# A block of hybrid layers, a two-way recurrence and routed experts on one core: layer fronts renewed, and the recurrence's products joined and reordered

## The chip, the core and the metric

The kernel runs on one core of a Trainium2 chip. The metric is the device time of one execution in microseconds (us), the median of several runs. TensorE (PE) multiplies matrices into PSUM banks, VectorE (DVE), ScalarE (ACT) and GpSimd (POOL) work on what lies in SBUF and PSUM, and SyncE (SP) issues most DMA transfers. Each engine executes its own instructions in order, and semaphores tie them together.

## What is computed

Two hybrid layers (convolution, retention and windowed attention over 256 tokens of width 1024), a mixer with a recurrence over a context and a latent sequence of 256 tokens each, and 32 experts. What the change touches is the head of each layer and the recurrence:

```python
def rms_norm(x, g):
    xf = x.astype(jnp.float32)
    y = xf * lax.rsqrt(jnp.mean(xf * xf, axis=-1, keepdims=True) + EPS) * g.astype(jnp.float32)
...
def hybrid_layer(x, ...):
    h = rms_norm(x, norm_g)
    z = h @ w_in
...
def wkv_bidir(r, k_d, v, kk, w, a, state0):
    ...
    def step(s, inp):
        r_t, w_t, k_t, v_t, aa_t, bb_t = inp
        sa = jnp.einsum('dbhij,dbhj->dbhi', s, aa_t)
        s = s * w_t[..., None, :] + sa[..., :, None] * bb_t[..., None, :] + v_t[..., :, None] * k_t[..., None, :]
        y_t = jnp.einsum('dbhij,dbhj->dbhi', s, r_t)
        return s, y_t
    state, ys = lax.scan(step, state0, xs)
```

The recurrence has 8 heads of 64 and two directions (d). It runs over the context first, and its final states start the latent one.

## The kernel before

All is float32. A loop over two layers (hybrid_tensor, hybrid_scalar, hybrid_pool, hybrid_vector, hybrid_loads; one function per engine) is followed by the mixer and then by a loop over experts. Weights come in units of 2 MB (1024 x 512) through a ring of three buffers, issued by SyncE in the order in which TensorE uses them. The order on every engine is that of the code; nothing is scheduled by a planner.

**The front of a layer.** ScalarE squares xT in four pieces, TensorE sums the squares with a matrix of ones (L305), ScalarE takes the root (L532), VectorE the reciprocal (L699), and eight operations scale xT into hT (L706), one per 128 features. After the last of them h_ready rises, and TensorE begins the first unit of the projection (features, L265). Between the sums and this unit TensorE has the products of ada(0) (L231). ScalarE works by function tables; where the next function lies in another table, an ACT_TABLE_LOAD stands ahead of it. The parameters of a layer, par, are loaded by GpSimd at its start into one buffer (L659), after the last addition to xT of the layer before; ScalarE waits for them ahead of the root, because the exponential of lam (L527) reads them and stands there. All engines wait at the program's start for four transfers: xT, shared_cons, cons and mpar.

**The recurrence.** It goes by chunks of 64 tokens: four turns over the context (turns 0 to 3) and four over the latent (4 to 7). The tokens of a chunk are tied by a triangular system, which is inverted by doubling in five levels. All is done for two directions and four pairs of heads, so a product is a group of 16 matmuls of 64x64 (helper halves, L1381): for each of the four pairs c and each direction d the upper and the lower half of the partitions. both_ways issues it with d innermost. In most products direction 1 is turned: its upper half of partitions goes to the lower half of PSUM and the other way round. In g0_state, out_state and d0 it is not. Within the kernel's names:

- front: pairs (B by A, masked by VectorE into MP, L2124) and firsts (A by B, from which the first inverse is made, L2128 and L2131). The front of turn n + 1 is issued in turn n behind the product u, except at the change to the latent.
- a level k: t1 (T1 = level cut by X1, banks 0 and 1), copied by ScalarE (L1802), then d1 (banks 2 and 3), which VectorE adds to X1 (L2181), and d0 (banks 4 and 5), which accumulates X0 and which ScalarE copies (L1794). GpSimd makes the level cuts from MP (L1208).
- between(k) stands between t1 and d1: the products of keys, more, g0_state, g0_keys, state_keys and out_state. In latent turns a fill (beside: work of other parts, L1496 to L1509) follows, and TensorE waits for it.
- by_token: V, B and K of the chunk are transposed by products with the identity (L1423), ahead of t1 of levels 1, 2 and 3, into tV, tB and tK. VectorE copies V for it into sV (L2106).
- aside: in context turns ScalarE and VectorE do work for the latent part between the steps of a level.

Each t1, d1 and d0 waits for both directions of what it reads:

```python
    pe.wait_ge(g["levels_cut"].sem, g["levels_cut"].at(turn, 2 * k + 2))
    both_ways(t1(k), "t_done")
    between(k)
    ...
    pe.wait_ge(g["t_out"].sem, g["t_out"].at(turn, 2 * k + 2))
```

Of the kernel before, what the change touches and what calls it, by code (L numbers as in the profile page):

```python
# [13 lines left out]
DC = D // P  # L14
T = 256
# [135 lines left out]
def hybrid_signals(ctx, nc, g):  # L151

    for name, per, *more in (
        ("x_squared", 4), ("x_sum", 1), ("x_root", 1), ("conv_root", 1), ("ret_root", 4), ("qk_root", 5), ("h_ready", 1), ("dve_step", 120), ("pool_step", 4),
# [15 lines left out]
def hybrid_memory(ctx, nc, g):  # L170
# [13 lines left out]
    sb("par", [PAR_WIDTH])  # L184
# [24 lines left out]
def hybrid_tensor(pe, nc, g, l):  # L209
# [49 lines left out]
    def features(p, w, col, rhs=None, last=None):  # L259
# [252 lines left out]
def hybrid_scalar(act, nc, g, l):  # L512

    par = g["par"]
# [5 lines left out]

    for i in range(4):
# [3 lines left out]
    act.wait_ge(g["par_in"].sem, g["par_in"].at(l, 1))  # L525
    a = PAR["decay"]
    nc.scalar.activation(g["lam"][:, :], par[:, a:a + 8], ACT.Exp).then_inc(  # L527
        g["lambda_ready"].sem, g["lambda_ready"].one())
# [8 lines left out]
    root(rows[:, 0, :], stat[0], D, "x_root")  # L537
    act.wait_ge(g["decay_sum"].sem, g["decay_sum"].at(l, 1))
# [114 lines left out]
def hybrid_pool(pool, nc, g, l):  # L653
# [4 lines left out]
    pool.wait_ge(g["y_out"].sem, g["y_out"].at(l, 0))  # L658
    pool.dma_start(g["par"][:, :], g["par_dram"][bass.ds(l, 1), :, :].rearrange("o p n -> (o p) n")).then_inc(  # L659
        g["par_in"].sem, g["par_in"].one())  # L660
# [19 lines left out]
def hybrid_vector(dve, nc, g, l):  # L680
# [9 lines left out]
    par, step, rows, sm = g["par"], g["dve_step"], g["rows"], g["small"]  # L690
# [13 lines left out]
    dve.wait_ge(g["par_in"].sem, g["par_in"].at(l, 1))  # L704
# [4 lines left out]
    ins.then_inc(g["h_ready"].sem, g["h_ready"].one())  # L709
# [238 lines left out]
def hybrid_loads(sp, nc, g, l):  # L948

    for n, (kind, u) in enumerate(SEQUENCE):  # L950
# [16 lines left out]
        else:  # L967
# [4 lines left out]
            g["landed"][n % RING].sem, g["landed"][n % RING].one())  # L972

# [85 lines left out]
def mixer_signals(ctx, nc, g):  # L1059
    for name, per, *more in (  # L1060
# [5 lines left out]
        ("first_done", 1), ("x_ready", 2), ("levels_cut", 2 * LEVELS), ("t_done", 2 * LEVELS), ("t_out", 2 * LEVELS), ("x1_turned", 2), ("x0_set", 2), ("x0_done", 2 * LEVELS), ("x0_out", 2 * LEVELS),  # L1066
# [11 lines left out]
def mixer_memory(ctx, nc, g):  # L1078
# [38 lines left out]
    for name, width in (("sA", 3), ("sB", 1), ("sK", 1), ("sV", 1), ("tB", 1), ("tK", 1), ("tV", 1), ("MP", 1), ("MQ", 1), ("NQ", 2),  # L1117
# [1900 lines left out]
```

## Time and profile before

| what | value |
|---|---|
| runs | 2692.95, 2689.22, 2692.46 us, median 2692.46 |
| profiled execution | 2685.37 us, its span 2683.5 us |
| granted TensorE clock, mean | 0.991 |
| PE busy | 2552.9 us, 95% of the span |
| DVE, ACT, POOL busy | 927.9, 582.7, 150.0 us |
| first layer, projection to its end | 24.5 to about 654 us |
| second layer | to about 1302 us |
| mixer up to the recurrence | to about 1417 us |
| recurrence | to 1646 us |
| experts and end | to 2683.5 us |

The profile is one execution. A matmul in float32 is shown as two records, so a group of the recurrence has 32 records. Busy time counts a matmul until its modelled end, some 0.2 us after its issue, so a short wait is shown shorter than it is. "Issue" as the end of a wait means that nothing the profile shows was waited for.

### The profile page before, as it was taken

What the parts mean: (1) busy time and instruction counts of PE and PEld (TensorE: products, weight loads), DVE (VectorE), ACT (ScalarE), POOL (GpSimd) and SP (SyncE); (2) the same over time, 40 slices, a digit from 0 to 9 for tenths busy, and PEclk for the clock granted to TensorE, in tenths of its full rate; (3) what the DMA queues carried; (4) which work ended last, traced back from release to release, by engine and by line L of the source; (5) the groups of instructions that cost most, each with busy time, mean ns of one, the idle gap of its engine ahead of it and who ended that gap; (6) DMA issues with size and microseconds to landing.
All of it is one profiled execution on the core that took longest, in us unless ns stands there. A gap on an engine that the chain in (4) does not pass through costs nothing.

```text
span 2683.5 us, 42917 instructions
## 1 busy us (share of the span) xinstructions
PE 2552.9 (95%) x18398; PEld 1678.9 (63%) x18398; DVE 927.9 (35%) x2019; ACT 582.7 (22%) x1166; POOL 150.0 (6%) x125
## 2 busy tenths in 40 slices
PE   7999999998999999999997788899999999999998
PEld 6866887887885887888886677433333333333333
DVE  1763363312186345322465754411111111111112
ACT  2100233300100123220234533311111111111112
POOL 0050000000023000000002321000000000000000
PEclk9999999999999999999999999999999999999999
DMA  6546232344445432326420002899999999999996
GB/s 233 209 168 212 102 126 95 126 157 159 157 167 209 165 108 103 125 95 215 170 83 3 4 4 97 369 428 428 428 429 428 428 428 428 428 428 428 428 429 254
DMA packets 135048, 636.18 MB, mean 237 GB/s; under 512 B 5136, under 2 KB 5408, under 8 KB 109152
## 3 DMA queue, kind: packets, MB, share of 16 engines
q1 hardware_dynamic: 133904, 629.78, 59.0%
q0 software_dynamic: 1008, 4.37, 0.4%
q8 instruction: 112, 1.84, 0.3%
q14 instruction: 24, 0.20, 0.0%
HBM read 633.08 MB, written 1.05 MB: 236 GB/s over the span
## 4 chain that ended last, share of the span: by engine, by line
PE 93%; ACT 3%; DVE 2%; issue 1%; DMA 1%; SPq 0%; ACTq 0%; DVEq 0%
PE bank L265 26%; PE bank L2550 17%; PE bank L2578 9%; PE bank L455 6%; PE bank L477 4%; PE bank L286 4%; PE bank L1332 4%; PE bank L1381 4%; PE bank L2512 2%; PE bank L2541 2%; PE bank L2498 2%; PE bank L1625 1%; PE bank L353 1%; PE bank L2570 1%; ACT hidT L2661 1%
## 5 line engine op out<-in xcount | busy, mean ns | idle before, releaser
L265 PE MATMUL bank<-hT,ring 128*128 128x256 f32 x3136 | 695.0, 382 | 12.9 <-DVE hT L706 12.9
L265 PEld LDWEIGHTS bank<-hT,ring 128*128 128x128 f32 x3136 | 596.5, 191 | 106.8 <-DVE hT L706 14.7
L2550 PE MATMUL bank<-ring,hsel 128*64 128x512 f32 x2112 | 461.8, 595 | 0.0
L2550 PEld LDWEIGHTS bank<-ring,hsel 128*64 128x64 f32 x2112 | 149.0, 137 | 310.9 <-issue 310.6
L2823 DVE TENSOR_SCALAR glu<-bank 128x256 f32<-128x256 f32 x66 | 28.0, 425 | 754.6 <-PE bank L2550 751.2
L2578 PE MATMUL bank<-ring,hidT 128*64 128x512 f32 x1024 | 226.8, 595 | 22.0 <-ACT hidT L2661 22.0
L739 DVE SCALAR_TENSOR_TENSOR a_buf<-v_pad,par,a_buf 128x256 f32<-128x256 f32 x480 | 215.8, 532 | 0.0
L2578 PEld LDWEIGHTS bank<-ring,hidT 128*64 128x64 f32 x1024 | 70.5, 137 | 156.2 <-issue 128.1
L1381 PE MATMUL bank<-ring 64*64 64x64 f32 (+1 forms) x5888 | 136.1, 225 | 28.9 <-issue 13.4
L1381 PEld LDWEIGHTS bank<-ring 64*64 64x64 f32 x5888 | 123.2, 137 | 43.6 <-issue 16.2
L2652 ACT ACTIVATE sig<-glu 128x256 f32<-128x256 f32 x66 | 27.5, 417 | 458.8 <-DVE glu L2823 458.8
L286 PE MATMUL bank<-ring,hT 128*128 128x512 f32 x256 | 111.4, 594 | 0.0
L477 PE MATMUL bank<-ro,ring 128*128 128x256 f32 x512 | 111.4, 379 | 0.0
L477 PEld LDWEIGHTS bank<-ro,ring 128*128 128x128 f32 x512 | 97.0, 190 | 13.8 <-issue 0.8
L1332 PE MATMUL bank<-stack,ring 128*128 128x256 f32 x480 | 105.4, 381 | 0.0
L1332 PEld LDWEIGHTS bank<-stack,ring 128*128 128x128 f32 x480 | 91.8, 191 | 13.2 <-issue 0.7
L286 PEld LDWEIGHTS bank<-ring,hT 128*128 128x128 f32 x256 | 48.2, 190 | 60.0 <-issue 60.0
L1208 POOL TENSOR_TENSOR ring<-ring,mcons 128x256 f32<-128x256 f32 x80 | 62.4, 814 | 254.8 <-DVE ring L2124 254.8
L2664 ACT ACTIVATE ye<-bank 128x512 f32<-128x512 f32 x33 | 19.7, 597 | 237.2 <-PE bank L2578 237.2
L2512 PEld LDWEIGHTS bank<-selgT,ye 64*128 64x128 f32 x544 | 49.7, 186 | 33.0 <-issue 26.8
L2512 PE MATMUL bank<-selgT,ye 64*128 64x256 f32 x544 | 67.9, 389 | 0.8 <-ACT finrow L2666 0.8
L2498 PE MATMUL bank<-h_tok,sel 128*64 128x512 f32 x272 | 64.2, 592 | 0.5 <-DVE sel L2745 0.5
(425 smaller groups left out, 2477.4 us busy)
## 6 DMA issues: line engine op xcount, KB each, us to landing
ring<-in_w SPq DMA_DIRECT2D x196, 2048.0 KB, 16.7
ring<-in_w_in SPq DMA_DIRECT2D x66, 2048.0 KB, 7.8
ring<-in_w_ada SPq DMA_DIRECT2D x12, 2048.0 KB, 8.0
ring<-in_w_ret_out SPq DMA_DIRECT2D x8, 2048.0 KB, 8.0
ring<-in_w_out SPq DMA_DIRECT2D x6, 2048.0 KB, 8.5
ring<-in_w_conv_out SPq DMA_DIRECT2D x4, 2048.0 KB, 8.6
ring<-in_w_attn_out SPq DMA_DIRECT2D x4, 2048.0 KB, 8.0
extra<-in_w SPq DMA_DIRECT2D x2, 2048.0 KB, 34.9
```

The lines of the kernel that those rows point to most:

```text
L265: mm = nc.tensor.matmul(out[:, j, :], w[:, k, col + j * P:col + (j + 1) * P], rhs[:, k, :], start=(k == 0), stop=(k == DC - 1))
L286: mm = nc.tensor.matmul(out[:, :, :].rearrange("p a b -> p (a b)"), g["hT"][:, k, t * P:(t + 1) * P], w[:, k, :], start=(k == 0), stop=(k ...
L455: mm = nc.tensor.matmul(out[:, j, :], ws[k // DC][:, k % DC, cols + j * P:cols + (j + 1) * P], rhs[:, k, :], start=(k == 0), stop=(k == n ...
L477: mm = nc.tensor.matmul(out[:, j, :], w[:, k, col:col + P], g["ro"][:, row * DC + k, :], start=(row == 0 and j == 0 and k == 0), stop=(row ...
L739: ins = nc.vector.scalar_tensor_tensor(out=y[:, c, :], in0=v[:, c, t:t + T], scalar=w, in1=y[:, c, :], op0=ALU.mult, op1=ALU.add)
L1208: nc.gpsimd.tensor_tensor(g["cut"][:, k, d * NC:(d + 1) * NC, :], g["MP"][:, d * NC:(d + 1) * NC, :], row(mask[:, k, d, :], NC), ALU.mult) ...
L1332: mm = nc.tensor.matmul(flat[(q + 3) % 4][:, 0:T], w[:, k, j * P:(j + 1) * P], g["stack"][:, k, lo:lo + T], start=(k == 0), stop=(k == DC ...
L1381: mm = nc.tensor.matmul(out[at:at + 64], lhsT[lo:lo + 64], rhs[lo:lo + 64], start=start, stop=stop, skip_group_check=not (start and stop))
L2498: mm = nc.tensor.matmul(half(flat[6], side), g["sel"][:, t, :], g["h_tok"][:, t, side * UNIT:(side + 1) * UNIT], start=(t == 0), stop=(t = ...
L2512: mm = nc.tensor.matmul(g["bank"][b][:, at, :], half(g["ye"], side)[:, n * P:(n + 1) * P], half(g["selgT"], side), start=False, stop=last, ...
L2550: mm = nc.tensor.matmul(half(flat[4 + b], side), g["hsel"][:, 2 * (j % 2) + k, j // 2, :], w[:, at:at + UNIT], start=False, stop=(j == 3 a ...
L2578: mm = nc.tensor.matmul(half(flat[7], side), g["hidT"][:, c, j, :], w[:, at:at + UNIT], start=(j == 0 and c == 0), stop=(j == 1 and c == 3))
```

## The change

In the layers: par of both layers is loaded once, at the start, into a tile twice as large. Cons is loaded behind the second unit of weights, and the first who read it wait for it alone. ScalarE takes the squares first, then Silu of the condition, then loads the square-root table by an unread element; in layer 1 that stands ahead of the squares. The exponential of lam goes behind the root. h_ready rises once per scaled piece, and TensorE waits for each piece in the first half of the first unit.

In the recurrence: the matrix "eye" is put beside A (turner), so that the pair products have 128 columns and give B by token in their second half, and in context turns the keys products give K likewise. by_token stays for V (read from m_v directly) and, in latent turns, for K. The pairs and the firsts lie in different banks, MP waits for the pairs alone, and the firsts stand behind the wait for U. t1, d1 and d0 are issued one direction after the other, each with its own waits. tB has two buffers, because it is filled before the turn before has ended with it.

```diff
@@ hybrid_tensor
             for k in range(DC):
+                if p == 0 and j == 0:
+                    pe.wait_ge(g["h_ready"].sem, g["h_ready"].at(l, k + 1))
                 mm = nc.tensor.matmul(out[:, j, :], w[:, k, col + j * P:col + (j + 1) * P], rhs[:, k, :],
...
-    pe.wait_ge(g["h_ready"].sem, g["h_ready"].at(l, 1))
     for u in range(R_GATE):
+        if l == 0 and u == 1:
+            pe.wait_ge(g["cons_in"].sem, g["cons_in"].at(None, 1))
@@ hybrid_scalar
+    if l:
+        root_table()
     for i in range(4):
...
-    act.wait_ge(g["par_in"].sem, g["par_in"].at(l, 1))
+    if l == 0:
+        nc.scalar.activation(g["cond"][:, :, 0:2], g["mpar"][:, MIX_PAR["cond"]:MIX_PAR["cond"] + 2 * DC].rearrange(
+            "p (c s) -> p c s", s=2), ACT.Silu).then_inc(g["cond_ready"].sem, 1)
+        root_table()
...
+    act.wait_ge(g["x_sum"].sem, g["x_sum"].at(l, 1))
+    root(rows[:, 0, :], stat[0], D, "x_root")
+    act.wait_ge(g["par_in"].sem, g["par_in"].at(None, 1))
     a = PAR["decay"]
@@ mixer_tensor
+    def one_way(product, d, signal):
+        for c in range(NC):
+            mm = product(d, c)
+        mm.then_inc(g[signal].sem, g[signal].one())
...
+            out = flat[d][:, c * 2 * C2:(c + 1) * 2 * C2].rearrange("p (k w) -> p k w", k=2)
+            return halves(out, g["sB"][:, dc, :], g["with_turner"](dc), turned=d == 1)
...
-            pe.wait_ge(g["levels_cut"].sem, g["levels_cut"].at(turn, 2 * k + 2))
-            both_ways(t1(k), "t_done")
+            for d in range(DIRS):
+                pe.wait_ge(g["levels_cut"].sem, g["levels_cut"].at(turn, 2 * k + d + 1))
+                if k:
+                    pe.wait_ge(g["x_next"].sem, g["x_next"].at(turn, 2 * (k - 1) + d + 1))
+                else:
+                    pe.wait_ge(g["tok_out"].sem, g["tok_out"].at(turn, d + 1))
+                one_way(t1(k), d, "t_done")
...
-            if k < LEVELS - 1:
-                both_ways(d1, "d_done")
-            both_ways(d0(k), "x0_done")
+            for d in range(DIRS):
+                pe.wait_ge(g["t_out"].sem, g["t_out"].at(turn, 2 * k + d + 1))
+                if k:
+                    pe.wait_ge(g["x0_out"].sem, g["x0_out"].at(turn, 2 * (k - 1) + d + 1))
+                if k < LEVELS - 1:
+                    one_way(d1, d, "d_done")
+            for d in range(DIRS):
+                one_way(d0(k), d, "x0_done")
...
         if keep_state and turn != STEPS - 1:
-            front(turn + 1)
+            pairs(turn + 1)
         pe.wait_ge(g["u_out"].sem, g["u_out"].at(turn, 2))
+        if keep_state and turn != STEPS - 1:
+            firsts()
@@ mixer_scalar
+        for d in range(DIRS):
+            act.wait_ge(g["pairs_out"].sem, g["pairs_out"].at(turn, d + 1))
+            nc.scalar.activation(g["tB"][turn % 2][:, d * NC:(d + 1) * NC, :],
+                                 flat[d].rearrange("p (n w) -> p n w", n=NC)[:, :, C2:2 * C2], ACT.Copy)...
...
-                act.wait_ge(g["t_done"].sem, g["t_done"].at(turn, 2 * k + 2))
+                act.wait_ge(g["t_done"].sem, g["t_done"].at(turn, 2 * k + d + 1))
@@ mixer_vector
-                v.tensor_copy(g["sV"][:, h, :], g["m_v"][:, :, s])
...
+        for d in range(DIRS):
+            dve.wait_ge(g["paired"].sem, g["paired"].at(turn, d + 1))
+            v.tensor_tensor(g["MP"][:, d * NC:(d + 1) * NC, :], ...)
         dve.wait_ge(g["first_done"].sem, g["first_done"].at(turn, 1))
@@ hybrid_pool, hybrid_loads and program
-    pool.wait_ge(g["y_out"].sem, g["y_out"].at(l, 0))
-    pool.dma_start(g["par"][:, :], g["par_dram"][bass.ds(l, 1), :, :]...)
+            pool.dma_start(hyb["par"][:, :, :], shared["par_dram"].rearrange("l p n -> p l n"))...
...
+        if l == 0 and n == 1:
+            sp.dma_start(g["cons"][:, :], g["cons_dram"][:, SHARED_CONST:CONST_WIDTH])...
```

Three places show what moves. The first is TensorE at level 2 of the first context turn. Before, t1 goes to banks 0 and 1 and d1 to banks 2 and 3, two matmuls to each bank in turn:

```order
L1381 MATMUL bank0<-ring 64x64 [waits levels_cut,x_next]
L1381 MATMUL bank0<-ring 64x64
L1381 MATMUL bank1<-ring 64x64 x2
...
L1381 MATMUL bank6<-ring 64x64 [waits state_ready]
...
L1381 MATMUL bank2<-ring 64x64 [waits x0_out,t_out]
L1381 MATMUL bank2<-ring 64x64
L1381 MATMUL bank3<-ring 64x64 x2
```

And now, the same t1 and d1, and d0 in banks 4 and 5:

```order
L1405 MATMUL bank0<-ring 64x64 [waits x_next,levels_cut,tok_out]
L1405 MATMUL bank0<-ring 64x64 x7
L1405 MATMUL bank1<-ring 64x64 [waits x_next,levels_cut]
L1405 MATMUL bank1<-ring 64x64 x7
L1405 MATMUL bank6<-shift,ring 64x64 [waits tok_out,state_ready]
...
L1405 MATMUL bank2<-ring 64x64 [waits x0_out,t_out]
L1405 MATMUL bank2<-ring 64x64 x7
L1405 MATMUL bank3<-ring 64x64 [waits x0_out,t_out]
L1405 MATMUL bank3<-ring 64x64 x7
L1405 MATMUL bank4<-ring 64x64 x8
L1405 MATMUL bank5<-ring 64x64 x8
```

The products of direction 0 stand together ahead of those of direction 1, and each direction waits for its own copies; the group of g0_state stays between them.

The second is TensorE in front of the first unit of a layer; L231 and L232 are ada(0), L265 and L268 the projection. Before:

```order
L305 MATMUL bank<-b_buf,shared_cons 128x256
L231 MATMUL bank<-ring,cond 32x512 [waits landed0,cond_ready]
L231 MATMUL bank<-ring,cond 32x512 x7
L265 MATMUL bank<-hT,ring 128x256 [waits landed1,h_ready]
L265 MATMUL bank<-hT,ring 128x256 x31
```

And now:

```order
L308 MATMUL bank<-b_buf,shared_cons 128x256
L232 MATMUL bank<-ring,cond 32x512 [waits landed0,cond_ready]
L232 MATMUL bank<-ring,cond 32x512 x7
L268 MATMUL bank<-hT,ring 128x256 [waits h_ready,landed1]
L268 MATMUL bank<-hT,ring 128x256 [waits h_ready] x7
L268 MATMUL bank<-hT,ring 128x256 x24
```

The first eight matmuls each wait for their piece of hT, where one wait for all pieces stood.

The third is ScalarE at the start of the program: squares (b_buf), Silu (cond), exponential (lam) and root (rows). Before:

```order
L2950 ACT_TABLE_LOAD [waits start_in]
L2950 ACTIVATE cond<-mpar 128x8x2 [waits eps_set]
L523 ACTIVATE b_buf<-xT 128x512 [waits y_out] x4
L527 ACT_TABLE_LOAD
L527 ACTIVATE lam<-par 128x8 [waits par_in]
L532 ACT_TABLE_LOAD
L532 ACTIVATE rows<-bank,eps 128x256 [waits x_sum]
```

And now:

```order
L532 ACT_TABLE_LOAD [waits y_out,start_in]
L532 ACTIVATE b_buf<-xT 128x512 [waits eps_set]
L532 ACTIVATE b_buf<-xT 128x512 [waits y_out] x3
L535 ACT_TABLE_LOAD
L535 ACTIVATE cond<-mpar 128x8x2
L526 ACT_TABLE_LOAD
L526 ACTIVATE unread<-eps 1x1
L541 ACTIVATE rows<-bank,eps 128x256 [waits x_sum]
L549 ACT_TABLE_LOAD
L549 ACTIVATE lam<-par 128x8 [waits par_in]
```

The squares come first, the root needs no parameters, and the load of its table stands ahead of the wait for the sums.

## Rows read from the trace of the kernel before

**Rows 1.** The page, part 4, the chain of waits by engine.

```profile
PE 93%; ACT 3%; DVE 2%; issue 1%; DMA 1%; SPq 0%; ACTq 0%; DVEq 0%
```

**Rows 2.** The chain in order of time, first front: start us, us, what.

```profile
2.11 8.38 DMA mpar<-in_mpar_dram
...
10.56 1.28 ACT L2950
...
12.73 6.06 PE bank L305 x16
...
21.19 3.27 DVE hT L706 x8
...
24.50 15.67 PE bank L265 x64
...
70.54 14.01 PE bank L265 x64
```

**Rows 3.** Transfers issued in the first 5 us: KB, us to landing.

```profile
ring<-in_w_in SPq DMA_DIRECT2D x1, 2048.0 KB, 17.9
cons<-in_cons_dram SPq DMA_DIRECT2D x1, 1473.0 KB, 8.5
```

**Rows 4.** Windows: us, busy of PE, PEld, DVE, ACT, POOL, clock, DMA share, GB/s.

```profile
5.00:12.00 7.00, 0.00 (x0) 0.00 (x0) 0.00 (x0) 1.43 (x3) 0.00 (x0) 1.00 1.02 408
...
667.50:673.00 5.50, 5.44 (x13) 4.36 (x14) 4.33 (x9) 1.10 (x1) 0.00 (x0) 0.51 0.00 0
```

**Rows 5.** The chain, front of the second layer.

```profile
654.24 6.11 DMA par<-in_par_dram
...
661.89 0.48 ACT rows L532
...
664.25 3.27 DVE hT L706 x8
...
667.56 16.68 PE bank L265 x64
```

**Rows 6.** Timeline of both fronts: start us, us, engine, line, operation, idle before.

```profile
3.44 17.62 SPq L971 DMA_DIRECT2D ring<-in_w_in  x3
...
653.04 3.62 PE L305 MATMUL bank<-b_buf,shared_cons 128*128 128x256 f32 x16
...
656.59 1.92 PE L231 MATMUL bank<-ring,cond 128*32 128x512 f32 x16
```

**Rows 7.** Waits of PE, 1420 to 1650 us: us in total, times, longest.

```profile
PE bank L1444 <- DVE ring L2131: 14.4, 7, 2.5
PE bank L1381 <- issue: 14.2, 21, 1.2
```

**Rows 8.** Timeline of PE, end of turn 0: d0, u, three groups.

```profile
1443.21 1.15 PE L1381 MATMUL bank<-ring 64*64 64x64 f32 x32 [0.28 <-ACT ring L1802]
1445.00 0.69 PE L1381 MATMUL bank<-ring 64*64 64x64 f32 x32 [0.64 <-ACT ring L1794]
...
1447.55 1.63 PE L1381 MATMUL bank<-ring 64*64 64x64 f32 x96
```

**Rows 9.** Timeline, latent turn 6: t1 with keys, d1 with d0, t1 with more.

```profile
1591.39 1.55 PE L1381 MATMUL bank<-ring 64*64 64x64 f32 x63
...
1594.06 1.48 PEld L1381 LDWEIGHTS bank<-ring 64*64 64x64 f32 x64 [0.46 <-PE bank L1505]
...
1595.92 1.15 PE L1381 MATMUL bank<-ring 64*64 64x64 f32 x63
```

**Rows 10.** The chain in context turn 2: t1, t1, T1 copies, u.

```profile
1484.83 0.69 PE bank L1381 x32
...
1488.66 0.77 PE bank L1381 x32
...
1489.45 0.66 ACT ring L1802 x2
...
1499.33 1.71 PE bank L1381 x94
```

More of the change, by code:

```diff
@@ L183, in hybrid_memory @@
     sb("pair", [2, T])
[L184 removed]
+    sb("par", [DEPTH, PAR_WIDTH])
+    sb("unread", [DEPTH])
     sb("cons", [CONST_WIDTH - SHARED_CONST])
@@ L512, in hybrid_scalar @@
 def hybrid_scalar(act, nc, g, l):
-    par = g["par"]
+    par = g["par"][:, l]
     def take(p, out, func):
@@ L537, in hybrid_scalar @@
     root(rows[:, 0, :], stat[0], D, "x_root")
+    act.wait_ge(g["par_in"].sem, g["par_in"].at(None, 1))
+    a = PAR["decay"]
+    nc.scalar.activation(g["lam"][:, :], par[:, a:a + 8], ACT.Exp).then_inc(
+        g["lambda_ready"].sem, g["lambda_ready"].one())
     act.wait_ge(g["decay_sum"].sem, g["decay_sum"].at(l, 1))
@@ L688, in mod_take @@
                                 bias, ALU.add).then_inc(g["mod_part"].sem, g["mod_part"].one())
-    par, step, rows, sm = g["par"], g["dve_step"], g["rows"], g["small"]
+    par, step, rows, sm = g["par"][:, l], g["dve_step"], g["rows"], g["small"]
     stat = [g["bank"][7][:, 0, :], g["bank"][3][:, 0, :]]
@@ L1396, in chunk, with pairs, product, firsts @@
         return flat[bank][:, at + c * C2:at + (c + 1) * C2]
[L1398 to L1400 removed]
+    def pairs(turn):
+        def product(d, c):
             dc = d * NC + c
[L1402 to L1404 removed]
+            out = flat[d][:, c * 2 * C2:(c + 1) * 2 * C2].rearrange("p (k w) -> p k w", k=2)
+            return halves(out, g["sB"][:, dc, :], g["with_turner"](dc), turned=d == 1)
+        pe.wait_ge(g["staged"].sem, g["staged"].at(turn, 1))
+        both_ways(product, "paired")
+    def firsts():
+        def product(d, c):
             dc = d * NC + c
[L1406 to L1410 removed]
+            return halves(chunk(4 + d, c, NC * C2), g["sA"][:, dc, 0:C2], g["sB"][:, dc, :], turned=d == 1)
+        both_ways(product, "first_done", True)
     def step(turn):
@@ L1417, in step @@
         new_col = C2 * (1 + turn % 2)
+        token = [chunk_start(lat, i, d) for d in range(DIRS)]
         def by_token(name):
@@ L1532, in between @@
                 pe.wait_ge(g["state_ready"].sem, g["state_ready"].at(turn, 0))
+                if not lat:
+                    pe.wait_ge(g["tok_out"].sem, g["tok_out"].at(turn, 6))
                 both_ways(g0_state, "g0_done", True)
@@ L1596, in step @@
         if turn == STEPS - 1:
-            front(turn + 1)
+            pairs(turn + 1)
+            firsts()
     pe.wait_ge(g["p_out"].sem, g["p_out"].at(None, CTX_CHUNKS + 20))
@@ L1602, in mixer_tensor @@
     lora(1, 1, 6)
-    front(0)
-    g["first_done"].n = 0
+    pairs(0)
+    firsts()
+    g["first_done"].n = g["paired"].n = 0
     for turn in each_turn(g, 2 * STEPS, SCAN):
@@ L1804, in step @@
             for d in range(DIRS):
-                if 1 <= k < 4:
-                    nc.scalar.activation(direction(("tV", "tB", "tK")[k - 1], d), flat[d][:, NC * C2:2 * NC * C2],
+                if k == 1 or k == 2 and lat:
+                    nc.scalar.activation(direction(("tV", "tK")[k - 1], d), flat[d][:, NC * C2:2 * NC * C2],
                                          ACT.Copy).then_inc(g["tok_out"].sem, g["tok_out"].one())
+            for d in range(DIRS):
+                if k == 1 and not lat:
+                    act.wait_ge(g["pairs_out"].sem, g["pairs_out"].at(turn, d + 3))
+                    nc.scalar.activation(g["tK"][:, d * NC:(d + 1) * NC, :],
+                                         flat[6 + d].rearrange("p (n w) -> p n w", n=NC)[:, :, C2:2 * C2], ACT.Copy).then_inc(
+                        g["tok_out"].sem, g["tok_out"].one())
                 if k == 3:
@@ L2938, in _ @@
         def _(pool):
+            pool.dma_start(hyb["par"][:, :, :], shared["par_dram"].rearrange("l p n -> p l n")).then_inc(
+                hyb["par_in"].sem, hyb["par_in"].one())
             for l in each_turn(hyb, DEPTH, layer_names):
```

101 lines of the change are left out of this document (50 added, 51 removed).

## Prediction

> **What bounds the kernel now.** I read the chain of waits first. TensorE holds 93% of it [rows 1], so a change pays where TensorE waits, and costs wherever it gives TensorE work that nothing hides. The change touches two kinds of place: the front of each of the two hybrid layers, and the recurrence of eight turns (four context, four latent). Everything behind the recurrence, the expert loop above all, is not touched; it is TensorE's own work there and only moves with its start.
>
> The chain in order of time shows the first front. The last of four transfers lands at 10.49, ScalarE loads a table and makes squares, TensorE sums them (6.06), then root, reciprocal and eight scalings of hT (3.27) follow, and only then does the first projection start, at 24.50. It takes 15.67 where a later one of the same 64 records takes 14.01 [rows 2]. In the second layer the sums end at 653.04 + 3.62 = 656.66 and the state-conditioning products at 656.59 + 1.92 = 658.51, but the chain runs through the par transfer (to 660.35), a table load and the root at 661.89, and the projection starts at 667.56 and takes 16.68 [rows 5, 6]. The windows say why it is slow: a granted clock of 0.51, so mostly the level of 1.2 GHz, after 9 us in which TensorE did nothing [rows 4].
>
> In the recurrence the waits of TensorE are of three kinds: 14.4 us in all for the start of a turn (VectorE's L2131), 14.2 us called issue, in which it waits for nothing shown, and a few us inside the levels [rows 7].
>
> **Layer fronts.** First layer. The start no longer waits for cons (1473 KB), though par grows by a second layer's 128 x 330 numbers, 165 KB. The transfers run at about 408 GB/s [rows 3, 4]: 1308 KB less is 3.3 us (3.2 at 408, a little more at the later 390), so mpar lands at 7.2. ScalarE's first load (1.28) moves to the squares; Silu and its load now stand behind the squares, under the 6.06 of the sums. The sums begin 3.5 us earlier and end at 15.3; root and reciprocal follow, and hT begins at 17.7 instead of 21.19. TensorE now waits for one of the eight scalings (3.27 / 8 = 0.41) instead of all. Each later one takes 0.41 and TensorE uses 14.01 / 32 = 0.44 for one matmul, so it doesn't catch up. It starts at 18.15, 6.35 earlier. Its weights were issued at 3.44 and landed 17.9 later, at 21.3, behind all of cons [rows 3, 6]; with the 3.3 us they come at 18.0, just in time. TensorE's pause before it shrinks from 3.9 to 1 us, so I take the warm price: 15.67 - 14.01 = 1.66. Together 8.0. Cons lands about 4 us after these weights, near 22; VectorE, which then stands before the decays, and GpSimd wait for it, but TensorE needs it only before the second unit, near 32. If that cover were gone each us late would cost one.
>
> Second layer. par is there, and the square-root table is loaded before the squares. The root starts at 656.7 instead of 661.89 (5.2), and the wait for one scaling instead of eight is 2.86 less: 8.0. The pause falls from 9 us to 1, so the clock should not fall: 16.68 - 14.01 = 2.7. Together 10.7. Both fronts: 18.7. Bounds: with both projections still cold 14.4; with 1 us more at the first front 19.7.
>
> **Recurrence: what a group of products costs.** A group is 16 matmuls of 64x64, shown as 32 records. One alone takes 0.69, three in a row 1.63 [rows 8], so a further one costs (1.63 - 0.69) / 2 = 0.47. These groups alternate the directions, and the second is turned: it reads the lower half of the partitions and writes the upper one. The row of 1.15 for 32 records is the product d0, in which no direction is turned [rows 8]: 0.46 more, so 0.93. In the alternating order four quarters of the array are used in turn, in d0 only two. Issued direction by direction, the products T1 (t1) and d1 use two quarters for eight matmuls and then the other two. So I price each at 0.93 too: +0.46 for five t1 and four d1 in a turn, 4.2 us of TensorE's time. I cannot see the new order in this trace; the bounds are 0 (as fast as alternating) and 0.46 each, and d0 is by far the nearest row.
>
> By a rule of the Trainium skill (TensorE: Matmul & The Clock Gate, Part 3 on packing small matmuls) weight loads overlap running matmuls only if their row group differs. Both orders alternate the row groups equally, so by it the new order costs nothing. This trace speaks against it: d0 alternates row groups too and takes 1.15 against 0.69 [rows 8]. TensorEngine Tiling (Array Packing), Key Properties, says that different tiles run in parallel, and the trace agrees with that.
>
> Taken out: one transposing group per turn for B (now the second half of the pair products) and one more for K in context turns: -0.47 and -0.93. Wider products: the pairs in every turn and the keys in context turns have 128 columns instead of 64. The stretch with one wide group takes 1.55, the same count of narrow records 1.15 [rows 9]: +0.4 each.
>
> **Latent turns.** TensorE's queue is full there: between the products stand the fills, and after a fill and 0.46 of waiting for it come d1 and d0 (1.48 of weight loads), then at once the next groups [rows 9]. The scalar copy of T1 has long been made, so its earlier start buys nothing, and every group added is paid: +4.2 - 0.47. At the last level d0 by direction lets the scalar copies start earlier: -0.2. Sum +3.55 per turn, +14.2 for four; at most 4 x 4.2 = 16.8.
>
> **Context turns.** TensorE waits there. Turn 2 takes from the first t1 of level 1 (1484.83) to the product u (1499.33) 14.5 us, 3.6 per level [rows 10]. A level was a chain: t1, both T1 copies, d1, two additions of VectorE with other work between them. With the directions apart, one direction's copy and addition lie beside the other's products, and the queue of TensorE sets the pace: level 1 has t1 0.93 + d1 0.93 + d0 0.93, less 0.47 that starts early, plus 0.26 of waiting for the second copy. That wait is from the rows too: the copies start 0.79 after t1, 0.32 after its last issue, and one takes 0.66 / 2; after t1 of both directions (0.93) that is 0.93 + 0.32 + 0.33, while TensorE is busy until 0.93 + 0.47 with t1 and the first d1. It leaves about 0.2, with the hand-over 0.26. Level 1 comes to 2.6; level 2 the same groups and g0_state at 0.93: 3.7; level 3 with g0_keys 3.3; level 4 to u 3.0. That is 12.6, 1.9 less than 14.5. But the issue gaps, 14.2 / 8 = 1.8 per turn [rows 7], and the table loads of ScalarE's side work stay, and a queue that is full hides them less. I keep 1.0 per turn, -4.0 for four; bounds -7.6 and 0.
>
> **Start of a turn.** TensorE waited 14.4 / 7 = 2.1 us for it [rows 7]. The masks of the pair products (MP) leave this chain: two operations, 0.75. But the pairs are 0.4 longer and the first products now stand behind the wait for U, so VectorE starts the MP at about the same time and ends them when the first products are done. Worth 0.15 in a context turn; in latent turns the new copies of tB, behind the copies of y, take it back. The two copies of V per stage go from VectorE, 0.4 at the entry, the only place where they bound something. 0.4 for that, 0.15 for the three later context turns: -0.8 in all.
>
> **Sum.** -18.7 - 0.8 - 4.0 + 14.2 = -9.3. The profiled execution took 2685.37 (span 2683.5 and 1.9 around it), so it would be 2676.1. The median of the runs is 2692.46, 7 higher, and is what a later median compares with: 2683.2.
>
> **Rivals.** (1) Slower: the queue of TensorE is the bound in context turns too. Per turn it gains 9 x 0.46 - 0.93 + 0.8 = +4.0 of work. For it: issue gaps already last as long as the turn starts. Against it: d1 waits for the T1 copies, a gap of at least 1 us per level of which the profile shows only the end. If nothing hides it, +16.0 + 14.2 - 19.5 = +10.7: 2703. It decides from a loss of 1.3 us per context turn. (2) The fronts give less: the weights of the first unit land later than 18.0, since cons and the longer par share the engines, or the clock falls all the same. Worth 12 to 13 instead of 18.7: 2689, no measurable change. (3) The order by direction costs nothing, by the rule above. Then latent turns gain 0.5 to 0.7, and in context turns a level falls to about 2.5 (t1 0.23, copy, d1 0.23, addition with their delays twice 0.9), 5 us a turn: -19.5 - 2.5 - 20 = -42: 2650. Against it stand the 1.15. (4) Context turns give all of their 1.9 and changes of direction overlap a little, -3.6 and some 2 more: 2678.
>
> **How the numbers follow.** My forecast 0.64, own range 2678 to 2689; (1) 0.12; (2) 0.12; (3) 0.04; (4) 0.08. About 0.2%, 5.4 us, is what a measurement of this kernel can tell. Faster: 0.59 of mine, all of (3) and (4), 0.04 of (2): 0.75. Same: 0.05 + 0.07 + 0.01: 0.13. Slower: 0.12. The range leaves out (3) and most of (1): 2670 to 2695.
>
> **What would show it.** In the changed profile the first projection should start near 18.1 and 667.56 - 16 = 651.5, both with about 14.0 for 64 records. In latent turns t1 and d1 should stand as 16 and 16 records in about 0.9, and the turns be 3 to 4 us longer; in context turn 2 the stretch from t1 of level 1 to u should be 13 to 14 us instead of 14.5 [rows 10]. I am wrong in the main step if 32 records issued by direction take the 0.69 of the alternating ones, and in the sign if context turns grow by more than 1.3 us.

## The result, and the profile after

| | before | changed |
|---|---|---|
| runs beside each other | median 2692.70 us | 2662.57, 2663.27, 2667.72, 2669.99, median 2665.49 us |
| ratio, 95% interval | | 0.9911 (0.9887 to 0.9936) |
| the same pair again, at another time | median 2690.0 us | median 2666.09 us, ratio 0.9907 (0.9891 to 0.9924) |
| profiled execution, span | 2685.37, 2683.5 us | 2662.57, 2660.7 us |

The before median of 2692.70 counts a fourth run of 10795.36 us; the other three (2692.95, 2689.22, 2692.46) have 2692.46. By the ratios the change brings 24.0 and 25.0 us (by the medians 27.2 and 23.9), where 9.3 were forecast. I read the profile in the order of the prediction. First the two fronts, in the chain of waits in order of time (start us, us, what):

```profile
2.80 15.28 DMA ring<-in_w_in
...
18.13 14.08 PE bank L268 x64
...
648.74 0.48 ACT rows L541
...
651.10 0.50 DVE hT L719
...
651.73 14.05 PE bank L268 x64
```

The first projection starts at 18.13 instead of 24.50, right behind its weights (18.08), the second at 651.73 instead of 667.56, and both take the warm 14.0 to 14.1 [rows 2, 5]. The par transfer and the seven other scalings have gone from the chain.

Second the waits of TensorE in the recurrence, 1398 to 1625 us (us in total, times, longest):

```profile
PE bank L1478 <- DVE ring L2192: 9.5, 6, 2.0
PE bank L1405 <- issue: 5.1, 11, 1.0
PE bank L1405 <- ACT ring L1844: 3.8, 8, 0.5
PE bank L1381 <- ACT ring L1866: 1.7, 1, 1.7
PE bank L1405 <- DVE ring L2242: 1.6, 2, 1.1
...
PE bank L1405 <- ACT ring L1866: 1.4, 1, 1.4
PE bank L1405 <- POOL ring L1232: 1.1, 2, 0.6
```

The issue gaps fell from 14.2 to 5.1 us, the starts of turns from 14.4 to 9.5 [rows 7]. New are the two waits for L1866, ScalarE's copy of K's transposes in context turns.

Third the turns. Here and below a turn is the distance between the first records of turn_x1 (L1444 before, L1478 in the changed kernel) in two turns; the latent part runs from the fifth turn's start to the output projection.

| us | context turns | sum | latent part |
|---|---|---|---|
| before | 27.30, 27.63, 24.59, 25.60 | 105.1 | 124.9 |
| changed | 23.79, 24.86, 27.53, 24.68 | 100.9 | 124.5 |
| changed, second profile | 25.49, 24.93, 28.44, 24.92 | 103.8 | 123.5 |

The latent turns were to become 14.2 us longer and are about 1 shorter. This is the term that was wrong by about 15 us; the others miss by less and partly against each other (see below). The timeline of TensorE shows why, at the same place of latent turn 6 as [rows 9] (start us, us, engine, line, operation): d1 and d0 behind the fill, then the transposes of V.

```profile
1568.05 0.38 PE L1539 MATMUL bank<-kk,wf 128*128 128x256 f32 x1
1568.49 1.68 PE L1405 MATMUL bank<-ring 64*64 64x64 f32 x62
1569.95 0.27 PE L1459 MATMUL bank<-shared_cons,m_v 64*64 64x64 f32 x2
...
1570.52 1.40 PE L1405 MATMUL bank<-ring 64*64 64x64 f32 x64
```

And before:

```profile
1594.06 1.56 PE L1381 MATMUL bank<-ring 64*64 64x64 f32 x62
1595.40 0.27 PE L1423 MATMUL bank<-shared_cons,ring 64*64 64x64 f32 x2
```

From the first product to the next group it is 1.46 instead of 1.34 us: 0.12 for the order by direction, where the prediction had 0.46. The row of 1.40 is t1 and the group more behind it, 1.15 before [rows 9]: 0.25.

### The profile page after: what moved, and what is told of

It reads as the page before. It is cut to its first block, busy times and chain, and to the rows that moved or that the text cites. A ratio compares the mean times of both kernels' runs of the same rounds, so it can differ in the third digit from the quotient of the medians.

```text
span 2660.7 us, 42254 instructions
## 1 busy us (share of the span) xinstructions
PE 2558.3 (96%) x18014; PEld 1686.6 (63%) x18014; DVE 925.7 (35%) x2004; ACT 589.0 (22%) x1168; POOL 149.5 (6%) x124
## 4 chain that ended last, share of the span: by engine, by line
PE 94%; ACT 2%; DVE 2%; DMA 1%; issue 1%; POOL 0%; SPq 0%; ACTq 0%; DVEq 0%
PE bank L268 26%; PE bank L2612 17%; PE bank L2640 9%; PE bank L459 6%; PE bank L1405 5%; PE bank L481 4%; PE bank L289 4%; PE bank L1356 4%; PE bank L2574 2%; PE bank L2603 2%; PE bank L2560 2%; PE bank L1675 1%; PE bank L357 1%; PE bank L2632 1%; ACT hidT L2723 1%
## 5 line engine op out<-in xcount | busy, mean ns | idle before, releaser
L268 PE MATMUL bank<-hT,ring 128*128 128x256 f32 x3136 | 689.8, 380 | 3.0 <-DMA ring<-in_w_in 1.8
L268 PEld LDWEIGHTS bank<-hT,ring 128*128 128x128 f32 x3136 | 593.4, 190 | 94.4 <-issue 13.3
L1405 PE MATMUL bank<-ring 64*64 64x64 f32 (+1 forms) x5696 | 147.0, 229 | 15.9 <-issue 4.8
L1405 PEld LDWEIGHTS bank<-ring 64*64 64x64 f32 x5696 | 135.7, 136 | 30.1 <-issue 9.2
L2714 ACT ACTIVATE sig<-glu 128x256 f32<-128x256 f32 x66 | 27.5, 417 | 462.3 <-DVE glu L2885 462.3
L1356 PEld LDWEIGHTS bank<-stack,ring 128*128 128x128 f32 x480 | 91.2, 190 | 12.6 <-issue 0.3
```

Of the source, the lines that this page charges most:

```text
L1356: mm = nc.tensor.matmul(flat[(q + 3) % 4][:, 0:T], w[:, k, j * P:(j + 1) * P], g["stack"][:, k, lo:lo + T], start=(k == 0), stop=(k == DC ...
L1405: mm = nc.tensor.matmul(out[at:at + 64], lhsT[lo:lo + 64], rhs[lo:lo + 64], start=start, stop=stop, skip_group_check=not (start and stop))
```

## The experiments

**Which part brings what.** Two kernels divide the change.

The fronts alone: the changed hybrid layers and loads, with the mixer of before.

> The change's edits to the hybrid layers' fronts and to the program's loads, with the mixer of before (transposes, pair products and order of the recurrence as before). Both theories: the first projection starts near 18.1 us and the second layer's near 651.7, the recurrence is entered 20 to 22 us earlier than before and its eight turns keep their lengths of before (105.1 us context, 117.1 us latent, within 1 us). Theory A (the change's gain beyond the fronts is real work saved in the recurrence, some 5 us): ratio to before 0.9930, about 2673. Theory B (the recurrence gave nothing and the rest is where the clock falls): ratio as of the changed kernel, 0.991, about 2666 to 2669.

Measured: 2673.28 us median of 5, ratio 0.9939 (0.9925 to 0.9952). The recurrence begins at 1405.56 instead of 1424.02, 18.5 us earlier; its context turns take 107.1 us, its latent part 125.8. So the 18.7 of the prediction are there; I had expected an entry 20 to 22 us earlier, and the turns of before within 1 us, and the context turns took 2.0 more. (The 117.1 of the expectation end at 1646, the 124.9 of the table at the output projection.) The whole gains 16 us, and the mixer brings the rest. Theory A had put this at 0.9930, within the interval, and B's 0.991 lies outside.

All but the order by direction:

```
-            for d in range(DIRS):
-                pe.wait_ge(levels_cut ... 2 * k + d + 1) ...
-                one_way(t1(k), d, "t_done")
+            pe.wait_ge(levels_cut ... 2 * k + 2) ...
+            both_ways(t1(k), "t_done")
...
+                both_ways(d1, "d_done")
+            both_ways(d0(k), "x0_done")
```

> The changed kernel with t1, d1 and d0 of every level issued again in alternation of the two directions, behind waits for both directions; all else as changed. Theory P (that of the prediction: a group of 32 records by direction costs 0.47 us more than an alternating one): each latent turn is 9 x 0.47 = 4.2 us shorter than in the changed kernel, 17 us over four, each context turn 1 to 2.5 us longer: ratio to before about 0.987. Theory A (only 0.12 to 0.25 us a group where the products start fresh): latent turns 1.1 to 2 us shorter each, of which a part goes again in waits for both directions; context turns 1 to 2.5 us longer: sum -2 to +6 us against the changed kernel, ratio 0.990 to 0.993.

Measured: 2666.05 us median of 5, ratio 0.9915 (0.9901 to 0.9928); context turns 106.4 us, latent part 123.7. Theory P needed some 10 us less than the changed kernel; it falls. Against the fronts alone the joined transposes, copies and masks bring 6.5 us (their intervals overlap a little), 2.1 of them in the latent part (125.8 to 123.7) and 0.7 in the context turns; the rest I can't place, since the two profiled executions are only 4.1 us apart. TensorE's issue gaps fall by 8.7, but in the context turns its waits for VectorE take most of that back (windows of the two kernels' context turns, then of their latent parts, for the fronts alone):

```profile
PE bank L1399 <- issue: 8.9, 12, 1.0
PE bank L1462 <- DVE ring L2149: 8.8, 4, 2.5
...
PE bank L1399 <- issue: 8.5, 10, 1.4
```

and with the joined transposes, directions in alternation:

```profile
PE bank L1405 <- DVE ring L2239: 10.4, 13, 1.9
PE bank L1478 <- DVE ring L2189: 7.2, 4, 2.0
PE bank L1405 <- issue: 3.9, 8, 0.8
...
PE bank L1405 <- issue: 4.8, 7, 1.1
```

The order by direction then takes away what stands on top there: TensorE's waits for the additions of VectorE (x_next), 10.4 us in 13 times, are 1.6 to 1.9 in 2 or 3 in both profiles of the changed kernel. In the context turns of the profiles it brings 2.6 us (106.4 to 103.8, both with a granted clock of 0.95 there). In the whole time it brings nothing that can be measured: 0.9915 without it, 0.9911 and 0.9907 with it.

**Is it accumulation that makes d0 slow?** After the first profile I believed that a pair of quarters used again and again is slow only where products add to their bank, as d0 does. Two kernels test it, one in which t1 and d1 add too (start=False; their values are others), and one in which d0 starts fresh:

```
-            return halves(chunk(2 + d, c), g["XX"]..., g["T1"]..., turned=d == 1)
+            return halves(chunk(2 + d, c), g["XX"]..., g["T1"]..., False, True, d == 1)
```

```
-            return lambda d, c: halves(chunk(4 + d, c), g["T1"]..., g["XX"]..., False, k == LEVELS - 1)
+            return lambda d, c: halves(chunk(4 + d, c), g["T1"]..., g["XX"]...)
```

> Changed kernel, but the products t1 and d1 add to what stands in their bank instead of starting fresh (their values are other ones). Order, tiles, waits and counts are the same. Theory T-acc (a pair of tiles used again and again is slow, 0.93 us for 32 records, only where the products accumulate): t1 and d1 by direction go from about 0.6 to 0.93 us a group, each latent turn +9 x 0.34 = 3 us, all eight turns +18 to +25 us. Theory T-pair (d0 is slow for another reason, its tiles' pace does not hang on accumulation): turns within 2 us of the changed kernel in all.

> Changed kernel, but d0 starts fresh at each level instead of adding to its bank (its values are other ones). Theory T-acc: d0 goes from 0.93 to about 0.6 us a group of 32 records, five groups a turn: each latent turn 1.2 to 1.7 us shorter, all eight turns 8 to 13 us shorter. Theory T-pair: d0 stays at 0.93 us and the turns within 2 us in all.

Measured for the d1 and d0 of the same level, t1 and d1 adding:

```profile
1574.59 1.68 PE L1405 MATMUL bank<-ring 64*64 64x64 f32 x62
1576.06 0.27 PE L1459 MATMUL bank<-shared_cons,m_v 64*64 64x64 f32 x2
```

and d0 fresh:

```profile
1569.13 1.68 PE L1405 MATMUL bank<-ring 64*64 64x64 f32 x62
1570.60 0.27 PE L1459 MATMUL bank<-shared_cons,m_v 64*64 64x64 f32 x2
```

Both are those of the changed kernel to 0.01 us, and the latent parts 124.5 and 123.3. T-acc falls. (Their whole times, one run each, 2727.37 and 2747.09, don't compare: the other values give the experts more work, 2240 and 2304 records of its first matmul instead of 2112.)

**What the order costs in the array.** So I looked at how many records are under way together. Windows of 0.17 to 0.18 us through d1 and d0 (us, busy and, in brackets, the records that touch the window; a record is drawn 0.22 long, so each counts in two or more). By direction, from 1568.48:

```profile
1568.48:1568.65 0.17, 0.16 (x4) 1.00 0.00 0
...
1568.83:1569.01 0.18, 0.18 (x19) 1.00 0.00 0
1569.01:1569.18 0.17, 0.17 (x20) 1.00 0.00 0
1569.18:1569.36 0.18, 0.18 (x19) 1.00 0.00 0
1569.36:1569.53 0.17, 0.17 (x16) 1.00 0.00 0
1569.53:1569.70 0.17, 0.17 (x12) 1.00 0.00 0
```

In alternation (before):

```profile
1594.22:1594.40 0.18, 0.18 (x21) 1.00 0.00 0
1594.40:1594.58 0.18, 0.18 (x26) 1.00 0.00 0
1594.58:1594.75 0.17, 0.17 (x19) 1.00 0.00 0
1594.75:1594.92 0.17, 0.17 (x13) 1.00 0.00 0
```

Two quarters alone show 12 to 13, all four 26, and by direction, where the pairs change, 19 to 20. The starts of the single records give the rule for these products, which I call Q: a quarter takes one record every 58.4 ns, whatever the order and whether it adds or not. Sixteen records of a direction, eight for each of its two quarters, need 0.467 us; but the next direction, on the other two quarters, starts 0.295 after it (1568.488, 1568.783, 1569.077), while three of the eight steps are still to come. d0 is slow because both its directions use the same two quarters: 16 steps, 0.93.

Two kernels put a price on that in time. Both issue t1 of the latent turns twice, one changing quarters each time, the other only once:

```
 abab:  for d: t1(d)      then  for d: t1(d)
 aabb:  for d: t1(d), t1(d)
```

> The changed kernel with t1 of every level of the four latent turns issued twice, in the order direction 0, direction 1, direction 0, direction 1 (the second pass writes the same values again). Both kernels of this pair add the same 32 records a level, 20 levels in all. Theory Q (each quarter takes a record in 58.4 ns, and a direction on the other two quarters starts when three of the eight steps before it are still to come, so 0.295 us after it): +0.59 us a level, 2.9 a turn, +11.8 us in the latent turns. Theory P (32 records by direction cost 0.93 us whatever the order): +18.6 us.

> As the kernel beside it, but t1 issued twice in the order direction 0, 0, 1, 1: the same records, and the pair of quarters changes once instead of three times. Theory Q: each direction's second eight steps stand behind its first in the same quarters, +0.93 us a level, 4.7 a turn, +18.6 us in the latent turns, 7 us more than its neighbour. Theory P: +18.6 us, no difference between the two.

Measured: ratios 0.9967 (0.9957 to 0.9976) and 0.9985 (0.9976 to 0.9995), 10 runs each, so 4.8 us apart; the latent parts are 140.5 and 141.4 us, 17.0 and 17.9 over the second profile of the changed kernel. As elapsed time neither theory fits both: Q had 11.8 and 18.6, P 18.6 twice. In the array it is as Q says. From t1 to g0_state (its first bank<-shift record) in turn 6, abab:

```profile
1590.63 1.34 PE L1405 MATMUL bank<-ring 64*64 64x64 f32 x58
1591.76 0.27 PE L1405 MATMUL bank<-shift,ring 64*64 64x64 f32 x2
...
1592.82 1.04 PE L1405 MATMUL bank<-shift,ring 64*64 64x64 f32 x29 [0.67 <-issue]
```

and aabb:

```profile
1587.77 1.69 PE L1405 MATMUL bank<-ring 64*64 64x64 f32 x58
1589.25 0.27 PE L1405 MATMUL bank<-shift,ring 64*64 64x64 f32 x2
```

1.13 against 1.48, 0.35 apart (Q: 0.34). Over 20 levels that is 7 us. The times show 4.8, uncertain by nearly 4 on either side, and the profiled latent parts 0.9; abab has 5.8 us of issue gaps there and aabb 1.9, so the traces differ by less. P's "no difference" is just outside what the times allow; the pace of the array, not they, decides against it. The sums over the latent part (us) say where the 5 us go that abab takes beyond Q: its products add 13.6 us of busy TensorE, 2 more than Q has, and its idle time grows by 3.4.

| latent part | length | TensorE busy | idle |
|---|---|---|---|
| changed, second profile | 123.5 | 113.0 | 10.5 |
| abab | 140.5 | 126.6 | 13.9 |
| aabb | 141.4 | 131.3 | 10.1 |
| split (next experiment) | 122.7 | 108.9 | 13.8 |

**Orders built on Q.** Three kernels ran beside the changed one. The first keeps the order by direction in context turns and alternates in latent ones. The second interleaves, in latent turns, d1 of direction 1 with d0 of direction 0, which use different quarters; the third does so in all turns:

```
+                    one_way(d1, 0, "d_done")
+                    for c in range(NC):
+                        mm = d1(1, c)
...
+                        mm = d0(k)(0, c)
```

> The changed kernel once more, beside the three that follow. Of the fronts alone 0.9939 and of the changed kernel with the two directions in alternation 0.9915 were measured on one chip, and the traces put the recurrence 5 us shorter by direction than in alternation. If that is real time, this runs at 0.9895 to 0.990; if the clock's dips in the routing after the recurrence take it away each time (4 us in the profiled execution), at 0.991 to 0.9915.

> The changed kernel with the order by direction in the context turns and t1, d1 and d0 in alternation, behind waits for both directions, in the latent turns. From the traces of the changed kernel and of the one in alternation throughout: context turns 100.9 us as changed, latent turns 123.7 instead of 124.5 us (start of the fifth turn to the output projection). So 0 to -1 us against the changed kernel. By the prediction's price (0.47 us a group) it would be -17 us.

> As the split order, but in the latent turns d1 of direction 0 stands alone, then d1 of direction 1 in alternation with d0 of direction 0, then d0 of direction 1. Theory Q (each quarter of the array takes one record in 58 ns; d1 of direction 0 and all of d0 use the same two quarters, so 24 records stand behind one another in each): the 64 records of d1 and d0 take 24 x 58.4 = 1.40 us, as in alternation (1.40) and 0.12 less than by direction (1.52), while the first d1 is done earlier: -0.5 to -2 us against the split order. Theory P (records of one direction at a time cost 0.93 us a group of 32): 0.47 us more at each of four levels, +7 us.

> The changed kernel with t1 by direction as changed, and in all eight turns d1 of direction 0 alone, then d1 of direction 1 in alternation with d0 of direction 0, then d0 of direction 1. Theory Q: d1 and d0 of a level take 1.40 instead of 1.52 us, 0.12 us at each of 4 levels, -0.5 us a turn, -2 to -4 us over the recurrence, unless the first d0, which now is done some 0.1 us later relative to d1, is what is waited for: then 0. Theory P: no change or slower, since each of these groups uses two quarters at a time.

| | median us | ratio, 95% | context turns | latent part |
|---|---|---|---|---|
| changed, again | 2666.09 | 0.9907 (0.9891 to 0.9924) | 103.8 | 123.5 |
| split | 2663.52 | 0.9904 (0.9887 to 0.9920) | 104.2 | 122.7 |
| interleaved, latent | 2662.52 | 0.9903 (0.9886 to 0.9920) | 103.7 | 122.7 |
| interleaved, all | 2665.39 | 0.9905 (0.9889 to 0.9922) | 105.4 | 125.7 |

No difference that can be measured; the changed kernel's 0.9907 lies between the two values that I had given. Going back to alternation in latent turns is worth 0.75 us of the trace (0.7 in the pair of profiles further up), not the 14 to 17 that P needs. That doesn't mean that the order costs the array so little. The windows of the latent part, the changed kernel and then split (us, TensorE busy, records, clock, DMA share, GB/s):

```profile
1509.00:1633.00 124.00, 113.03 (x3689) 1.00 0.08 24
1509.00:1631.00 122.00, 108.52 (x3677) 1.00 0.07 23
```

Over the whole latent part it is 113.0 against 108.9 (table above): by direction TensorE is busy 4.1 us longer, and 3.3 of that come out of its idle time, which is 13.8 us in alternation and 10.5 by direction. So the price in the array is real, and most of it fell into waits that were there anyway. The interleaving's -0.5 to -2 did not come, and in all turns the trace is slower by 2.2 us in the latent part, which I can't explain: the issue gaps in it are 4.5 us against 2.1.

**The turn that grew.** Context turn 2 (the third) was forecast at 13 to 14 us from t1 of level 1 to u, and 14.5 before [rows 10]. The chain of the changed kernel:

```profile
1456.65 0.69 PE bank L1405 x16
...
1457.76 0.55 ACT ring L1861 x2
1458.31 0.56 ACT ring L1866 x2
...
1459.00 1.66 PE bank L1381 x8
...
1473.47 1.82 PE bank L1405 x73
```

It is 16.8 (1473.47 - 1456.65). Eight low-rank products (L1381) use the bank that now holds K's transposes, and so stand behind four copies of ScalarE. TensorE idles 1.7 us, and right behind it the clock falls:

```profile
1457.00:1460.00 3.00, 1.33 (x19) 1.15 (x15) 0.31 (x1) 1.49 (x5) 0.00 (x0) 0.91 0.00 0
1460.00:1464.00 4.00, 4.00 (x110) 3.41 (x108) 1.96 (x4) 2.51 (x7) 0.00 (x0) 0.64 0.01 4
1464.00:1468.00 4.00, 3.97 (x164) 3.84 (x156) 2.63 (x6) 3.38 (x9) 0.00 (x0) 1.00 0.01 4
```

The columns are those of [rows 4]; 0.64 of the full clock is mostly the level of 1.2 GHz. The last two kernels move these products behind d0 of the level, in the changed kernel and in the interleaved one:

```
-                    pe.wait_ge(... tok_out ... 6)
-                    lora(1, 3, 6)
...
+            if k == 1 and turn == 2:
+                pe.wait_ge(... tok_out ... 6)
+                lora(1, 3, 6)
```

> The changed kernel, but the eight low-rank products that stand in level 1 of context turn 2 behind the wait for the K transposes (the new copies, L1866, 1.7 us of TensorE's idle time and then half the clock for 3.4 us) are issued behind d0 of that level, when the copies have long been made. If the new wait is why this turn grew from 24.6 to 27.5 us: the turn falls by 1.7 us, and by 3 where the clock also stays up; 0.998 to 0.999 of the changed kernel (0.9895 to 0.990 of before). If the products are then waited for themselves by ScalarE, whose copies stand behind them, the turn keeps its length.

> The kernel with d1 and d0 of the latent turns interleaved (0.9903 of before) and the same move of the eight products: the two are in different turns, so the sum of both: 0.989 to 0.990 of before, context turn 2 as in the kernel beside it, latent turns 122.7 us from the fifth turn's start to the output projection.

Measured: 2660.79 us, ratio 0.9895 (0.9878 to 0.9911), and 2661.37 us, 0.9896 (0.9880 to 0.9913). The turn takes 25.7 and 25.5 us instead of 27.5 and 28.4, and 15.0 from t1 to u. Its clock stayed up:

```profile
1450.00:1474.00 24.00, 19.50 (x740) 17.89 (x732) 17.77 (x42) 16.16 (x43) 8.05 (x10) 1.00 0.02 4
1474.00:1499.00 25.00, 21.09 (x776) 19.99 (x780) 16.91 (x39) 14.18 (x39) 7.72 (x10) 0.93 0.02 4
```

But in this profile it falls in the next turn (0.93), so that gain is not safe: the four context turns together take 100.4 us (and 99.0 in the second kernel), where the changed kernel's first profile has 100.9 with the same mean clock of 0.98. That the wait made the clock fall is not shown. And 15.0 from t1 to u is still more than the 14.5 of before. Instead of the copies the products' own readers now cost something in the chain:

```profile
1461.79 1.09 PE bank L1381 x8
...
1462.91 1.58 ACT early L1766 x4
```

These two are the fastest kernels that I found, 3 us under the changed kernel by the ratios; the intervals of the times overlap.

## Why the prediction was wrong

**The step that failed.** "Issued direction by direction, the products T1 (t1) and d1 use two quarters for eight matmuls and then the other two. So I price each at 0.93 too". The first sentence is right, and so is the pace of two quarters, 0.93 for 32 records. The second doesn't follow from it: t1 and d1 change quarters after each direction, d0 never does, and at each change three of eight steps run beside the next direction's. The nearest row was near in count and shape, but not in what it shares. With d1 and d0 it costs 0.12 a level, with t1 and the group behind it 0.25, and of this about 0.75 us came out in all four latent turns together, where 16.8 stood in the sum. By Q it is 6 us of the array (0.37 at four levels of four turns); TensorE is busy 4.1 us longer, and its idle time gives 3.3 of them back. So a second step failed too, "TensorE's queue is full there" and "every group added is paid": before, 15 us of the 124.9 were idle. Which wait each group fills is not traced. The test that I had named, 0.69 for 32 records by direction, could not decide it: one direction alone, 16 records, is drawn with 0.69 (the row at 1456.65), so both would be 0.98 by Q, an estimate (0.295 + 0.69), though the next group can start after 0.59 (1568.488 to 1569.077), and the forecast had 0.93.

**Latent turns.** Without the order they gain 2.1 us by the pair of kernels, where 4 x 0.67 = 2.7 stood. With 0.75 for the order the term is -1.4 and not +14.2. The sum with it is -18.7 - 0.8 - 4.0 - 1.4 = -24.9; the ratios say -24.0 and -25.0. That it fits so well is luck, as the stretches of the two profiles show (us against before; the last one is counted from the output projection to the end of the program):

| | to the recurrence | context turns | latent part | behind it | span |
|---|---|---|---|---|---|
| changed | -22.0 | -4.3 | -0.5 | +3.9 | -22.8 |
| changed, second profile | -18.3 | -1.3 | -1.5 | +6.4 | -14.7 |

The prediction had nothing for what is behind the recurrence, which "only moves with its start". It took 1029.4 us before and 1033.4 and 1035.8 in the two profiles. The granted clock of its first 100 us was 0.95, 0.91 and 0.88. As far as the rows show it isn't the change's doing: the changed kernel with its eight products moved took 1029.7, all but the order 1029.5, with 0.95.

**Fronts.** Right in start and price: 18.13 for 18.1, 651.73 for 651.5, 14.1 and 14.05 for 14.0, and 18.5 us at the entry of the recurrence with the fronts alone. In the first front two bounds were forecast 0.15 apart, the scaling (18.15) and the weights (18.0). In this profile it was the weights; hT was begun at 16.88, earlier than the 17.7 forecast. In the other kernels with these fronts the projection starts between 18.1 and 19.5, in some of them behind hT.

**Context turns.** -4.0 forecast, -4.3 and -1.3 in the two profiles of the changed kernel, -2.6 for the order at the same clock. The aabb kernel, whose context turns are those of the changed kernel, took 102.0 us at a clock of 0.97, where before took 105.1 at 0.97: -3.1. The mechanism (one direction's copy and addition beside the other's products) is in the rows: the waits for x_next nearly vanish. But the stretch by which I had priced it, t1 of level 1 to u in turn 2, went the other way, 16.8 and without the added wait 15.0 where 13 to 14 stood; the gain lies in turns 0, 1 and 3. (In that sum the 3.7 for level 2 is 0.2 more than its named terms, 2.6 and 0.93.) What I didn't see is the wait for the K copies in turn 2, which costs this turn 2 to 3 us and was in the kernel's code: an added wait ahead of the eight products, with ScalarE's four copies in front.

**Start of the turns.** -0.8 forecast; the waits there are 9.5 in 6 times instead of 14.4 in 7, 0.5 less each, so the term was too small; part of this came with the fronts alone (12.6 in 7). **Issue gaps.** I kept them at 14.2; they fell by 9. The kernels show where: most of it with the joined transposes (17.4 with the fronts alone, 8.7 with all but the order, 5.1 with it). It is a gain that no term had, though not one of 9 us: what went from the gaps came back in part as other waits or as busy time. The fronts-alone kernel has more of them than before (17.4 to 14.2), so some 3 us of them are chance.

**Rivals.** (3), the order costs nothing, had the right idea with 2650; it had context turns gain 20. The rule behind it (Trainium skill, TensorE: Matmul & The Clock Gate, Part 3: weight loads overlap running matmuls only if the row group differs) explains neither the 0.93 of d0 nor the 0.12 here. What the Trainium skill says under TensorEngine Tiling (Array Packing), Key Properties, that different tiles run in parallel, is what these rows show, with 58.4 ns a record as each tile's own pace. (1) and (2) did not happen. (4) had both ideas, more from the context turns and changes of direction that overlap, with too little for the second.

## What to carry to other kernels

Price small packed matmuls by tile: count the steps behind one another in each quarter of the array, 58.4 ns each here, and let the next group start early if it uses other quarters. Then ask what of that time falls into waits that are there already: here 4.1 us more of busy TensorE cost 0.75. When the nearest row is taken for an unseen order, ask whether it shares the cause and not only the shape, and keep the other bound likely. Look at each added wait for idle time of TensorE: here 1.7 us of waiting stood in front of 3 us at half the clock, though whether it caused them is not shown.

## What was not expected of the hardware

- A quarter (64x64 tile, float32, 64 columns) takes one record in 58.4 ns whether the product adds or starts fresh, and the next matmul on free quarters starts when three steps, six records, of those before it are still to run.
- Issue gaps don't follow the number of matmul records: 7168 before (3352 and 3816 in its two halves) and 6790 in the changed kernel came with 14.2 and 5.1 us of gaps, but aabb had 4.5 with 7428 and all but the order 8.7 with 6778. In the latent parts they are small where the directions stand apart (1.9 to 2.6 us) and larger where they alternate, wholly or in part (3.3 to 5.8). Why is open.
- The place where the clock falls moves by chance, and with it 1.5 to 3 us of the context turns, and 4 to 6 us behind the recurrence, of one profile. The context turns of the changed kernel (us, busy, records, clock) in its first profile:

```profile
1402.00:1503.00 101.00, 82.99 (x3102) 0.98 0.02 4
```

and in its second:

```profile
1406.00:1509.00 103.00, 84.89 (x3092) 0.95 0.02 4
```

The same program took 100.9 and 103.8 us there. A difference of this size between two single profiles is no effect by itself.
